# Gated scan of an eight-head mixer: the two state products and their key transposes move behind the factors of the levels

## What is computed

```python
def step(S, xs):
    qc, kc, vc, gc = xs
    b = jnp.cumsum(gc, axis=2)
    decay = jnp.exp(jnp.where(lower, b[:, :, :, None, :] - b[:, :, None, :, :], -jnp.inf))
    a = jnp.einsum('bhtk,bhtsk,bhsk->bhts', qc, decay, kc)
    o = jnp.einsum('bhts,bhsv->bhtv', a, vc) + jnp.einsum('bhtk,bhkv->bhtv', qc * jnp.exp(b), S)
    b_end = b[:, :, -1]
    S_new = (jnp.exp(b_end)[..., None] * S
             + jnp.einsum('bhsk,bhsv->bhkv', kc * jnp.exp(b_end[:, :, None] - b), vc))
    return S_new, o
```

## The kernel before

| k-step | events |
|---|---|
| A4 | differences 1, factors 0; the value transposes |
| A5 | differences 2, factors 1 |
| A6 | key transposes, forwards |
| A7 | `hg_a` 0, differences 3, factors 2; then a weight cast |
| B1 | `hg_a` 1, differences 4, factors 3 |
| B2 | state forwards |
| B3 | `hg_a` 2, differences 5, factors 4 |
| B4 | key transposes, backwards |
| B5 | `hg_a` 3, differences 6, factors 5 |
| B6 | `hg_a` 4, factors 6; state backwards |
| B7 | `hg_a` 5; then a weight cast |
| C1 | `hg_a` 6 |
| C3 | `hg_o` |

## Time and profile before

### The profile page before, as it was taken

How to read it: one execution, slowest core, us unless ns; L and a number is a source line. 1 busy time by engine, 2 the same in 40 slices (tenths; PEclk the granted TensorE clock), 3 DMA queues, 4 the chain that set the end, 5 groups by cost and what they waited for, 6 DMA issues and landing times.

```text
span 3419.4 us, 42904 instructions
## 1 busy us (share of the span) xinstructions
PE 3288.4 (96%) x17072; PEld 2701.6 (79%) x17072; DVE 1705.2 (50%) x2600; ACT 1320.7 (39%) x1999; POOL 385.0 (11%) x394
## 2 busy tenths in 40 slices
PE   8999999999998999988999999999999999999998
PEld 4888778888887877876888778887778788877787
DVE  6665668655524767676433334343343334433433
ACT  4555533212123656564322344333332334333422
POOL 0111110000001535342000000010100000020000
PEclk9999999999999999999999999999999999999999
DMA  5222224665512111112333232222223322222232
GB/s 202 84 65 81 73 90 142 203 201 187 185 54 68 52 47 50 44 44 69 95 99 99 80 107 74 74 87 74 71 78 98 100 81 74 68 87 80 64 94 89
DMA packets 108998, 317.70 MB, mean 93 GB/s; under 512 B 28160, under 2 KB 30848, under 8 KB 108288
## 3 DMA queue, kind: packets, MB, share of 16 engines
q1 hardware_dynamic: 108800, 314.95, 29.3%
HBM read 312.81 MB, written 2.10 MB: 92 GB/s over the span
## 4 chain that ended last, share of the span: by engine, by line
PE 81%; DVE 7%; ACT 4%; POOL 4%; issue 2%; DMA 0%; DVEq 0%; ACTq 0%; SPq 0%
PE bank L1107 20%; PE bank L1111 20%; PE bank L1108 20%; PE bank L1118 3%; PE bank L1122 3%; PE bank L1119 3%; PE bank L1352 1%; PE bank L1220 1%; PE bank L1230 1%; POOL hg_d L2302 1%; PE bank L1371 1%; DVE w_low L1797 1%; PE bank L1381 1%; PE bank L1247 1%; POOL hg_d L2299 1%
## 5 line engine op out<-in xcount | busy, mean ns | idle before, releaser
L1107 PE MATMUL bank<-h_high_lat,w_high 128*128 128x512 f32 x2742 | 1126.9, 411 | 53.7 <-ACT h_high_lat L1413 19.4
L1111 PE MATMUL bank<-h_low_lat,w_high 128*128 128x512 f32 x2742 | 1081.4, 394 | 1.6 <-DVE h_low_lat L1861 1.4
L1108 PE MATMUL bank<-h_high_lat,w_low 128*128 128x512 f32 x2742 | 1077.8, 393 | 0.0
L1797 DVE TENSOR_TENSOR w_low<-w_raw,w_high 128x1024 fp32r<-128x1024 f32 (+3 forms) x442 | 540.3, 1223 | 1047.1 <-ACT w_high L1433 1045.7
L1433 ACT CAST w_high<-w_raw 128x1024 fp32r<-128x1024 f32 (+3 forms) x442 | 452.1, 1023 | 1171.7 <-PE bank L1111 794.4
L1107 PEld LDWEIGHTS bank<-h_high_lat,w_high 128*128 128x128 f32 x2742 | 520.5, 190 | 162.7 <-issue 69.4
L1111 PEld LDWEIGHTS bank<-h_low_lat,w_high 128*128 128x128 f32 x2742 | 519.0, 189 | 123.2 <-DVE h_low_lat L1861 12.6
L1108 PEld LDWEIGHTS bank<-h_high_lat,w_low 128*128 128x128 f32 x2742 | 521.0, 190 | 80.6 <-issue 7.7
L1122 PE MATMUL bank<-h_low_ctx,w_high 128*128 128x256 f32 x795 | 225.3, 283 | 0.1
L1119 PE MATMUL bank<-h_high_ctx,w_low 128*128 128x256 f32 x795 | 225.3, 283 | 0.0
L1118 PE MATMUL bank<-h_high_ctx,w_high 128*128 128x256 f32 x795 | 225.2, 283 | 0.0
(11 more groups left out here) (284 smaller groups left out, 4348.2 us busy)
## 6 DMA issues: line engine op xcount, KB each, us to landing
w_raw<-in_w_in_dram SPq DMA_DIRECT2D x176, 512.0 KB, 3.5
w_raw<-in_ffn_in_dram SPq DMA_DIRECT2D x88, 512.0 KB, 3.6
w_raw<-in_ada_w_dram SPq DMA_DIRECT2D x80, 512.0 KB, 3.9
w_raw<-in_w_ada_dram SPq DMA_DIRECT2D x48, 512.0 KB, 4.4
w_raw<-in_hg_in_dram SPq DMA_DIRECT2D x40, 512.0 KB, 3.5
w_raw<-in_ffn_out_dram SPq DMA_DIRECT2D x32, 512.0 KB, 3.5
w_raw<-in_qkv_dram SPq DMA_DIRECT2D x24, 512.0 KB, 3.6
w_raw<-in_proj_ret_dram SPq DMA_DIRECT2D x16, 512.0 KB, 3.5
```

The costliest lines, as they stand in the source:

```text
L1107: e.matmul(lat_b, a, h[:, k, :], start=start, stop=False)
L1108: e.matmul(lat_b, b, h[:, k, :], start=False, stop=False)
L1111: done = e.matmul(lat_b, a, l[:, k, :], start=False, stop=stop)
L1797: e.tensor_tensor(w_lo[n % 2][:, 0:w], raw[slot][:, 0:w], w_hi[n % 2][:, 0:w].bitcast(F32), ALU.subtract).then_inc(s_lo, 1)
```

## The change

```diff
-KHAT, STATE = (2, 5), (4, 7)
+KHAT, STATE = (5, 8), (7, 9)
```

## The result

The changed kernel takes 3440.59 us (median of 4 runs, 3439.03 to 3442.72); the kernel before, in the same comparison, 3421.82 us (3420.38 to 3422.77). The ratio is 1.0061, with a 95% interval of 1.0049 to 1.0072. The profiled execution took 3439.03 us, against 3421.22: 17.81 us more.

What follows compares the result with a forecast made beforehand. PE was taken to be bound together with a loop of POOL's differences, an exponential and DVE's factors. Eight heads at 2.60 us gave 20.8 on 3421.22, so 3442.0, with 0.93 for the median 3443; range 3430 to 3454.

Steps and rivals of the forecast that it cites:

- What is removed: PE ahead of level 0: transposes gone, so longer waits there and at levels 1 and 2; level 3's wait goes.
- The loop: POOL's differences, exponential, DVE's factors and casts behind level 2: factors 4 at 1313.80, so PE waits at level 4 until 1313.93.
- rival 3: Clock falls from bunched waits: paid from waits before level 4, behind it 1 to 1.7 us a head; 3451 to 3457; chance 0.06.
- the sum: Whole scan stage: eight heads at 2.60 us each, 20.8 us slower in all.
- the sign: Within a head: a granted clock below 1.00 was listed among the things that would make the prediction wrong.
- The new wait at level 6: PE waits 0.5 us at level 6 for a bank held by the forward state's chain, now behind factors 6 on DVE.
- the low bound given for it: Eighth head, with lighter k-steps: given the same 2.60 us, with 2 to 3.5 as bounds.
- Rival 1: Waits vanish, factors 4 ready by 1312.6: loss under 0.86 us a head, 3426 to 3429; chance 0.06.
- Rival 2: Loop keeps its old pace as POOL and DVE slow each other: 3.1 to 4 us a head, 3448 to 3455; chance 0.18.
- Rival 4: Order does not reach the path, or it gains: 3418 to 3426; chance 0.04, half of it a gain.

Runs made afterwards that it cites:

- experiment 1: Changed kernel plus dummy 512-column matmuls, two ahead of level 0 and one ahead of level 1: 3448.41 us, ratio 1.0081 to the kernel before.
- experiment 2: Changed kernel with one empty slot moved from behind the levels to ahead of level 0: 3444.28 us, ratio 1.0067 to the kernel before.
- experiment 5: Three of POOL's four differences left out after the first two levels, exponential scaled by 0.001: changed kernel 3396.92 us, kernel before 3383.19 us.
- experiment 4: Kernel before with transposes at s = 4 and 6, states at 5 and 7: 3432.15 us; with three extra matmuls a head, 3419.85 us.
- Experiment 7: Two weight casts on DVE held back in heads 1 to 7: kernel before 3408.34 us (ratio 0.9966), changed kernel 3440.99 us (1.0059).

## Why the prediction was right

The forecast was 3443.0 and the time 3440.6, slower, as forecast. Point by point, with the head of before moved by 67.11 us:

| | predicted | measured |
|---|---|---|
| factors 2 ready | 1373.64 | 1373.62 |
| level 2 starts | 1373.77 | 1374.89 |
| factors 3 | 1376.42 | 1376.53 |
| factors 4 | 1380.91 | 1381.30 |
| level 4 starts | 1381.04 | 1381.45 |
| factors 5 | 1384.16 | 1384.63 |
| forward state's chain done | 1388.17 | 1388.09 |
| level 6 starts | 1388.26 | 1388.24 |
| `hg_o` starts | 1394.53 | 1394.45 |

**What is removed.** The wait for L2077 at level 3 is gone, and the early levels wait instead: 2.68 at level 0, where some 2.7 were forecast. Of the 1.4 and 0.9 forecast at levels 1 and 2, 0.30 and nothing are left in this head, because PE's slow work fills them (see the clock). Factors 2 are ready at the same distance from level 0, to 0.02 us.

**The loop.** Factors 4 are 7.68 behind factors 2, forecast 7.27. From the cast's start to factors 4 it took 4.85 instead of 4.55: the cast took 1.75 beside POOL's differences, where the stretch that gave the price held it at 1.21 (though POOL worked beside it there too), and the products behind it took 0.25 less. Experiments 1, 2 and 5 show that this loop is what level 4 waits for.

**The clock.** The prediction named the mechanism as rival 3 and gave it 0.06, and it named a granted clock below 1.00 in a head as a sign of being wrong. The fall does occur, in seven of the eight heads of the changed kernel, and the forecast's own price stood all the same, because it fell ahead of level 4, where the prediction says it "is paid from waits". Level 2 was 1.1 later than forecast; level 4 was 0.4 later, and that by factors 4. So the sum was right with a clock that I had held to be the less likely case, and the sign was too strict: it left out the condition that the rival has. The chance of a fall was too low; the condition, before or behind level 4, was right, and experiments 1 and 4 show both sides of it. The Trainium skill, "TensorE: Matmul & The Clock Gate" (section on the HAM clock gate), says that TensorE drops to half clock after idling; the trace agrees, with 0.50 behind the 2.68. Whether a fall costs anything is another question; for that one needs the wait behind it.

**The new wait at level 6** did not occur. It was forecast at 0.5, with PE there at 1387.75. Level 4 was 0.41 later, and PE took 6.79 from there to level 6 instead of 6.71, so that it arrived at 1388.24, just behind the end of the chain (1388.09). Two errors cancelled here, and that is luck: half a microsecond more ahead of level 4, and half a microsecond less at level 6. Experiment 7 brought the wait out, 0.26.

**The sum.** From the first level 0 to the seventh `hg_o` it is 381.63 us (1130.78 to 1512.41) against 364.17 (1130.25 to 1494.42): 17.46, or 2.49 a head, forecast 2.60. The eighth head, from the seventh `hg_o` to the eighth, takes 67.43 instead of 65.44, 1.99 more, at the low bound given for it. Together with 0.53 at the first level 0 that is 19.98 at the last `hg_o` (1559.86 and 1579.84), forecast 20.8. At the end of the span 17.8 are left. Of the 2.2 between, 1.66 were given back right behind the stage, where the kernel before lost time by the clock and the changed one, in the same code and with the same two waits ahead of it (2.65 and 2.05), did not. Before, then after:

```profile
1583.00:1585.00 2.00, 2.00 (x6) 1.62 (x5) 0.02 (x1) 0.63 (x1) 1.17 (x1) 0.50 0.48 180
```
```profile
1603.00:1605.00 2.00, 2.00 (x10) 1.67 (x9) 0.00 (x1) 0.63 (x1) 1.19 (x1) 1.00 0.46 182
```

By a wait further on (1595.69 in the one, 1614.01 in the other) the distance was down to 18.32. In the other profiled executions of these experiments the same stretch is slow in eight and fast in three, with either order, so that I don't count it as an effect of the order.

**The rivals.** Rival 1 needed factors 4 within 6.1 us of factors 2; even with both casts away they took 6.85. Rival 2 (the loop at its old pace, 3.1 to 4 a head) is out by 2.49. Rival 4 (no change, or a gain) is out by the ratio, 1.0049 at the least.

## What to carry to other kernels

Work that stands between two links of a loop across engines runs while the loop goes round; moved behind the loop, it lengthens the path. Here 3.02 us a head were added behind level 4, and 0.50 won ahead of it. In these runs a lowered clock had a price only where no wait stood behind it: look for the next wait before putting the busy time down as a loss, and try it with extra matmuls that fit into the wait. And when the path runs through another engine's queue, look in that queue for work that isn't due yet: holding back two casts gave 12 us, more than any order of the products did.

## What was unexpected of the hardware

- The granted clock did not follow from one wait alone. Behind the 2.6 at level 0 of the changed kernel it fell in all seven heads, 0.3 to 3.5 us behind level 0's start; behind 2.0 (experiment 2) in four heads of seven; behind 1.3 (the kernel before) in none. In experiment 1 a wait of 1.85 at level 4, with the same work around it, brought it down in every second head only.
- POOL and DVE slow each other, and by how much depends on how they happen to meet. DVE's cast took 1.75 in the changed kernel, while POOL's first difference beside it took 1.60 instead of 0.61; in the kernel before the cast took 1.21 beside a first difference of 1.53. DVE's two products of a level took 0.88 in all when POOL was idle and 1.2 to 1.7 beside it:

```profile
1377.08 1.60 POOL L2299 TENSOR_TENSOR hg_d<-hg_b 128x256 f32<-128x256 f32 x1
...
1381.38 0.61 POOL L2299 TENSOR_TENSOR hg_d<-hg_b 128x256 f32<-128x256 f32 x1 [0.63 <-DVE hg_x L2095]
```
```profile
1381.93 1.67 DVE L2093 SCALAR_TENSOR_TENSOR hg_x<-hg_d,lower_bound,hg_k 128x256 f32<-128x256 f32 x2
...
1385.26 0.88 DVE L2093 SCALAR_TENSOR_TENSOR hg_x<-hg_d,lower_bound,hg_k 128x256 f32<-128x256 f32 x2
```
